# One projection stage of a streaming encoder step: longer steps, an earlier start, and a different share of expert rows on TensorE

## The reference, cut to what matters

```python
h   = x @ w_in                           # q, k, v, gates
x   = LayerNorm(alpha*x + concat(A, B) @ w_out)
# PEER, for each frame: 8 heads, 16 experts each = 128 rows of two tables
sc = einsum('thpd,hpnd->thpn', q, sub_keys); s, i = top_k(sc, 16)
cand = s[:, :, 0, :, None] + s[:, :, 1, None, :]; top, sel = top_k(cand, 16)
g   = softmax(top)
hid = einsum('td,thkd->thk', xs, u_tab[eidx])
a   = g * gelu(hid)
y   = einsum('thk,thkd->td', a, v_tab[eidx])
x   = LayerNorm(alpha*x + y)
```

## Time and profile before

| | |
|---|---|
| median of 3 runs | 1878.59 us (1874.08 to 1881.85) |
| the profiled execution, its time | 1878.59 us |
| its span | 1876.8 us |
| TensorE busy | 1568.1 us, 84% |
| VectorE busy | 1283.8 us, 68% |
| GpSimd busy | 1249.9 us, 67% |
| data moved | 724.85 MB, mean 386 GB/s |
| gathers (queue q0) | 605.75 MB, 82.3% of the 16 engines' span |

### The profile page before, as it was taken

One profiled execution on the slowest core, in us unless ns is written; L12 is line 12 of the kernel. 1 busy time (PEld: TensorE's weight loads), 2 busy tenths in 40 slices (PEclk: granted clock), 3 DMA queues, 4 the chain that ended last, 5 costly groups with the idle time before them and its releaser, 6 DMA issues.

```text
span 1876.8 us, 19183 instructions
## 1 busy us (share of the span) xinstructions
PE 1568.1 (84%) x5552; PEld 825.0 (44%) x5552; DVE 1283.8 (68%) x2826; ACT 609.2 (32%) x1743; POOL 1249.9 (67%) x1199
## 2 busy tenths in 40 slices
PE   8999889979996879877897988887699777767777
PEld 7586445623563545522354553244356222222222
DVE  2279885578957775677787558986756987466543
ACT  1422462222222752223474222245422313122211
POOL 3017676666776775677777657776867777777771
PEclk9999989999998999989998989978899899989999
DMA  9899999998999999999999999999999999999995
GB/s 312 300 350 357 411 384 399 408 396 312 363 410 410 411 409 409 409 410 409 334 405 407 405 401 410 409 349 376 370 399 408 410 409 409 409 409 409 410 410 229
DMA packets 207552, 724.85 MB, mean 386 GB/s; under 512 B 25080, under 2 KB 32024, under 8 KB 207320
## 3 DMA queue, kind: packets, MB, share of 16 engines
q0 software_dynamic: 166720, 605.75, 82.3%
q1 hardware_dynamic: 40728, 117.87, 16.6%
HBM read 716.37 MB, written 7.74 MB: 386 GB/s over the span
## 4 chain that ended last, share of the span: by engine, by line
DMA 29%; POOL 28%; PE 26%; issue 11%; DVE 5%; ACT 1%; SPq 0%; DVEq 0%; POOLq 0%; ACTq 0%
DMA vbuf<-in_peer_v,idx 17%; POOL ubuf L1866 12%; POOL vbuf L1866 11%; PE acc L1058 8%; DMA ubuf<-in_peer_u,idx 5%; POOL wring L1866 3%; PE mixer L1035 3%; PE mixer L759 2%; PE mixer L930 2%; PE mixer L716 2%; POOL held L1866 2%; DMA wring<-in_c_k 2%; PE mixer L872 1%; DVE ubuf L1791 1%; DMA wring<-in_peer_v,idx 1%
## 5 line engine op out<-in xcount | busy, mean ns | idle before, releaser
L1058 PE MATMUL acc<-vbuf,diag 128*128 128x512 f32 x1176 | 599.7, 640 | 152.4 <-DMA vbuf<-in_peer_v,idx 146.7
L1866 POOL DMA_INDIRECT ubuf<-in_peer_u,idx x513 | 549.1, 1070 | 259.5 <-issue 142.1
L1866 POOL DMA_INDIRECT vbuf<-in_peer_v,idx x467 | 507.9, 1087 | 232.4 <-issue 115.3
L1791 DVE CUSTOM_DVE_ANT_0 ubuf<-ubuf,x 128x1024 f32<-128x1024 f32 x329 | 400.0, 1224 | 190.6 <-DMA ubuf<-in_peer_u,idx 187.1
L1058 PEld LDWEIGHTS acc<-vbuf,diag 128*128 128x128 f32 x1176 | 216.0, 200 | 451.7 <-issue 402.7
L1791 DVE CUSTOM_DVE_ANT_0 ubuf<-ubuf,mixer 128x1024 f32<-128x1024 f32 x184 | 223.7, 1218 | 128.1 <-DMA ubuf<-in_peer_u,idx 96.1
L1348 ACT ACTIVATE act_h<-hid 128x4 f32<-128x4 f32 x144 | 29.6, 206 | 525.3 <-DVE hid L1791 524.8
L1803 DVE SCALAR_TENSOR_TENSOR y_acc<-vbuf,coef,y_acc 128x1024 f32<-128x1024 f32 x121 | 155.4, 1285 | 19.9 <-DMA vbuf<-in_peer_v,idx 15.8
L1035 PEld LDWEIGHTS mixer<-stage,wring 128*128 128x128 f32 x1280 | 149.8, 193 | 17.5 <-issue 16.4
L1035 PE MATMUL mixer<-stage,wring 128*128 128x128 f32 x1280 | 151.1, 277 | 2.2 <-DMA wring<-in_w_pq 2.1
L1377 ACT ACTIVATE diag<-ident,coef 128x128 f32<-128x128 f32 x365 | 129.6, 395 | 8.8 <-PE acc L1058 4.8
(11 more groups left out here) (301 smaller groups left out, 2043.8 us busy)
## 6 DMA issues: line engine op xcount, KB each, us to landing
wring<-in_w_pq SPq DMA_DIRECT2D x80, 512.0 KB, 8.1
wring<-in_w_out SPq DMA_DIRECT2D x40, 512.0 KB, 7.4
wring<-in_w_qk SPq DMA_DIRECT2D x34, 512.0 KB, 6.7
ubuf<-in_peer_u,idx POOLq DMA_INDIRECT x513, 11.6
vbuf<-in_peer_v,idx POOLq DMA_INDIRECT x467, 11.6
wring<-in_w_v SPq DMA_DIRECT2D x12, 512.0 KB, 9.7
wring<-in_c_k SPq DMA_DIRECT2D x8, 512.0 KB, 6.3
wring<-in_c_v SPq DMA_DIRECT2D x8, 512.0 KB, 7.6
```

Source lines behind the costliest of these rows:

```text
L1058: last = pe.matmul(sums[hf], diags[D_PLAN[n][0]], v_buf[b][:, hf * 512:(hf + 1) * 512], start=first, stop=last_one)
L1791: nc.vector.tensor_tensor_reduce(out=u, in0=u, in1=x, scale=1.0, scalar=0.0, op0=ALU.mult, op1=ALU.add, accum_out=hid[:, k % MARKS:k % MAR ...
L1866: pool.indirect_dma_start(buf, None, a[table], bass.IndirectOffsetOnAxis(ap=idx[p % 2][:, at:at + 1], axis=0)).then_inc(landed_, 16)
```

## The change

Five things change, and all other code stays.

- Steps of the shared projection: 54 steps become 28. The gate is now one step instead of two, each value tile one step instead of two, each query/key tile one step instead of two.
- Inside a value step the loop over blocks is now outside and the loop over the tile's two input slices inside. The matmuls are the same; those of the 64 sample frames (64 columns of weights instead of 128) come once in a tile instead of twice.
- The stage's range goes from slots 93 to 146 to slots 82 to 144. The later stages of block 2 and `X_MID` start one or two slots sooner, and block 0's n stage two.
- `on_tensor` loses the rule for slots 93 to 145, where every second v row went to TensorE. The general rule holds there now: two of three. Counting by the function, TensorE gets 450 of the 576 v rows instead of 440, and VectorE ten fewer.
- ScalarE's and VectorE's parts of the stage get step numbers to match.

```diff
 def x_steps(p):
-    return {0: 13, 1: 13, SHARED: 54, 3: 2, SMP: 6}[p]
+    return {0: 13, 1: 13, SHARED: 28, 3: 2, SMP: 6}[p]
...
-    if 93 <= k < 146 or 339 <= k < 369:
+    if 339 <= k < 369:
         return k % 2 == 0
     lo, hi = ((62, 82), (70, 122), (51, 111), (41, 105))[p]
     return lo <= at < hi or k % 3 != 2
...
-          2: ((93, 146), (146, 181), (181, 194), (194, 210), (200, 251)),
+          2: ((82, 144), (144, 180), (180, 193), (193, 209), (199, 250)),
...
-X_MID = {1: 26, 2: 146, 3: 257}
+X_MID = {1: 26, 2: 144, 3: 257}
...
-        rows = (211.0, 324.0, 422.0, end + 4.0 + late, end + 4.0 + late)[p]
+        rows = (209.0, 324.0, 422.0, end + 4.0 + late, end + 4.0 + late)[p]
...
-                for c in range(2):
-                    k = 2 * (j % 4) + c
-                    for b, cols in enumerate(XCOLS.values()):
-                        at = (3 * hf + b) * 512
+                for b, cols in enumerate(XCOLS.values()):
+                    at = (3 * hf + b) * 512
+                    for c in range(2):
+                        k = 2 * (j % 4) + c
                         last = pe.matmul(mixer[0:cols.stop - cols.start, at:at + 512], xs[:, k, cols], w[:, c, :],
                                          start=k == 0, stop=k == KT - 1)
-                    if c == 1:
-                        last.then_inc(v_done, 1)
-                    yield
+                last.then_inc(v_done, 1)
+                yield
...
         def shared_scalar(act):
-                if t == 5:
+                if t == 3:
                     act.wait_ge(gate_z, SHARED + 1)
...
-                if t in (11, 19):
-                    hf = t // 8 - 1
+                if t in (6, 10):
+                    hf = t // 4 - 1
...
         def shared_vector(dve, chain):
-                if t == 3:
+                if t == 2:
                     dve.wait_ge(gate_done, SHARED + 1)
...
-                if t == 12:
+                if t == 6:
                     dve.wait_ge(gate_e, SHARED + 1)
                     dve.wait_ge(v_done, 8 * SHARED + 4)
```

More of the change, by code:

```diff
@@ L702, in shared_tensor @@
                 last = pe.matmul(ps_t[0:FOX_HEADS, 0:XN], wg[:, c, :], xs[:, c, :], start=c == 0, stop=c == KT - 1)
-                if c == KT - 1:
-                    last.then_inc(gate_done, 1)
-                if c % 4 == 3:
-                    yield
+            last.then_inc(gate_done, 1)
+            yield
             for j in range(8):
@@ L727, in shared_tensor @@
                     last = pe.matmul(mixer[:, at:at + XN], w[:, c, :], xs[:, c, :], start=c == 0, stop=c == KT - 1)
[L728 to L732, removed]
+                last.then_inc(qk_done, 1)
+                yield
+            for _ in range(x_steps(SHARED) - 9 - MATS):
                 yield
@@ L1081, in shared_scalar @@
             for t in range(x_steps(SHARED)):
-                if t == 5:
+                if t == 3:
                     act.wait_ge(gate_z, SHARED + 1)
                     nc.scalar.activation(gx[2], gx[1], ACT.Exp).then_inc(gate_e, 1)
-                if t == 14:
+                if t == 7:
                     act.wait_ge(gate_u, SHARED + 1)
                     nc.scalar.activation(gx[4], gx[3], ACT.Ln).then_inc(gate_l, 1)
-                if t in (11, 19):
-                    hf = t // 8 - 1
+                if t in (6, 10):
+                    hf = t // 4 - 1
                     act.wait_ge(v_done, 8 * SHARED + 4 * hf + 4)
@@ L1094, in shared_scalar @@
                     nc.scalar.copy(v_wait[:, cols], mixer[0:DEC, at + 2 * 512:at + 3 * 512]).then_inc(shared_out, 1)
-                n = (t - 23) // 4
-                if t % 4 == 3 and 0 <= n < MATS // 2:
+                n = (t - 12) // 2
+                if t % 2 == 0 and 0 <= n < MATS // 2:
                     act.wait_ge(qk_done, MATS * SHARED + 2 * n + 2)
@@ L1422, in shared_vector @@
                     nc.vector.tensor_scalar(u, e, 1.0, None, ALU.add).then_inc(gate_u, 1)
-                if t == 16:
+                if t == 9:
                     dve.wait_ge(gate_u, SHARED + 1)
@@ L1429, in shared_vector @@
                     link(nc.vector.reciprocal(t5, u))
-                if t == 18:
+                if t == 11:
                     link(nc.vector.tensor_tensor(l, l, t5, ALU.mult))
@@ L1434, in shared_vector @@
                     nc.vector.scalar_tensor_tensor(lf_wait, z, 0.0, l, ALU.min, ALU.subtract).then_inc(logf_done, 1)
-                if t == 20:
+                if t == 13:
                     dve.wait_ge(logf_done, SHARED + 1)
```

## The result

| | before | changed |
|---|---|---|
| median | 1876.34 us (4 runs, 1873.78 to 1881.85) | 1897.12 us (4 runs, 1896.46 to 1897.78) |
| profiled execution, time | 1878.59 us | 1893.44 us |
| its span | 1876.8 us | 1891.3 us |
| changed / before | | 1.0107, interval [1.0081, 1.0133] |

The changed kernel is about 20 us slower, 1.1%. The profiled execution shows 14.9 us of them. The forecast was 1892, range 1880 to 1903.

The account below looks back on a forecast made before the run. Gathers filling the DMA engines bound the kernel, so unfilled time is lost. Stage idle rises from 16.6 to 29.0 us (+12.4), plus 1 us jitter: 1876.8 + 13.4 = 1890.2 span, plus 1.8 outside, 1892 us; range 1880 to 1903.

Parts of the forecast that it names:

- The stall: Start of the shared projection: TensorE stands at the gate from 380.5 us until xs lands, taken as 400.
- When xs lands: Load of xs: packet turns with the gathers until these run dry at about 397, then 1.8 us for 1000 packets.
- TensorE's work: Shared projection from the gate on: 74.3 us for 18 slots plus 111.8 for 37, together 186.1 us.
- the clock: TensorE after some 20 us idle: a throttled clock adds 2 us, bounds 0 and 4.
- idle DMA: Stage window of 207.5 us less 178.5 of DMA work: 29.0 us idle, before 16.6, so +12.4 us.
- the queue that is worked off, 7.6 us: DMA work in the stage: issue-to-landing time falls from 15.6 us to 8, counted as 7.6 us of transfers.
- The hidden stall: Rival at the stage's start: 15.6 us of queued DMA covers the wait, xs lands by 385; 1876 us, chance 0.20.
- VectorE's relief: Second stretch of the stage: ten v rows fewer, 12.9 us of VectorE, worth 0 to 3.5 us, taken as 0.
- The filled free time: Rival before the stage: values fill TensorE's 10.4 idle us between 382 and 412.7; 13.9 us faster, 1865, chance 0.06.

Follow-up runs that it names:

- one load: Changed kernel with xs by one load from an input in the tile's order: 1879.07 us, 1.0025; same load in the kernel before: 1872.0 us, 0.9988.
- the start at 93: Changed kernel with the shared projection starting at slot 93 again, all else changed: 1.0158 in a first run, then 1884.85 us, 1.0055 in a second.
- the first occasion: First of three timing occasions for the experiments; every kernel was slower there, the kernel before took 1973.85 us.
- the kernel with eight loads: Changed kernel with xs by eight loads of 1280-byte pieces, 1024 packets instead of 3072; one execution, 1883.44 us.

## Why the prediction was right

**The stall, shown.** The gate began at 399.70 (400 forecast), and stage<-in_xT released the wait. The stall was taken away in two experiments (one load, the start at 93), shortened in two, and made alone in another. It is 13 to 15 of the 20 us.

**When xs lands, shown.** Turns by packet until the gathers are dry, then fast. From 396 to 397 us, at the start of the fast stretch, q1 passes 551 packets, most of them pieces of 256 bytes:

```profile
q1 hardware_dynamic: 551, 0.16, 73.9%
```

That is 73.9% x 16/551 = 21 ns of an engine each, no more than the 28 of the forecast.

**TensorE's work, right in its sum.** The chain of the changed kernel has 5.29 us for each value tile and 0.2 in the row behind it (5.5 forecast), 4.31 for a query/key tile, and the last of them started at 586.0 (588 forecast). The stage from the gate on took 186.7 us; the forecast was 188.1 with the clock. Its two halves were not split as forecast. The value half held 17 v rows and not 15: without the clock's 2.2 us it took 77.7 us instead of 74.3, and the second half 106.7 instead of 111.8. The gate took 6.71 us, at a granted clock of 0.50 until 404 (1.2 GHz of 2.4) and 0.95 behind it, against 4.47 us with one load, where TensorE came to it without the long wait: 2.2 us (2 forecast). The Trainium skill (TensorE: Matmul & The Clock Gate, Part 1) says that an idle array is throttled, and here the trace agrees.

**The term that was mis-sized.** I had 29.0 us of idle DMA for the stage, and the trace shows 36.2. The term "the queue that is worked off, 7.6 us" is the one. I had let the queue end at 8 us from issue to landing; it ended at 10.4, by the gathers of 560 to 586 us (median us from issue to landing):

```profile
ubuf<-in_peer_u,idx POOLq DMA_INDIRECT x10, 10.4
vbuf<-in_peer_v,idx POOLq DMA_INDIRECT x9, 10.4
```

And 57.85 MB of gathers were served from 381.2 to 586.4, 141.1 us at 410 GB/s, where I had 140.8 for 55 slots and 7.6 on top. In that time GpSimd issued 54 u and 54 v gathers of 0.524 MB, 56.6 MB. So 1.2 MB came out of the queue, 3.0 us and not 7.6, and the window held 54 slots and not 55, 2.6 us less. That times from issue to landing made too much of the queue is as I read it: the 15.6 us ahead of the stage had packets of xs in them, one for each of the gathers' own, and they are not all gathers still to be moved. It was not tried by itself. In full: the window was 205.2 us instead of 207.5; the gathers took 141.1 instead of 148.4 of it and the rest (11.42 MB, 27.9 us) instead of 30.1, since I had priced xs by its packets' time and not by its bytes; so 36.2 us are left. With 1.3 us more on the side of before, the profiled stage lost 18.3 us more than before, not 12.4. That the profiled execution came out at 1893.44, 1.4 us from the forecast, is luck to this extent: the stage lost some 5 us more than forecast, and the sample block's attention happened to take 5.6 us less than in the profile of before. The median is 5 us above the forecast.

**The hidden stall, wrong by the same term.** That rival had 1876 for no wait at all. With one load the gate began at 385.31, as in the rival, and the kernel came out at 1.0025: not under the kernel before, but slightly over it. Its two halves lost 16.7 + 1.6 = 18.3 us where the rival had 14. That the first 15 us of a stall are covered by the queue is true of the stall itself (2.3 us lost in it) and false of the whole: the value half behind it lost 31.0 us instead of 16.7. As I read it, it would have worked off the same queue, and found none. Per us of wait the stage lost 0.76 (5.2 us for 6.8) to 0.97 us (17.9 for 18.5).

**The ten rows.** The forecast had them inside its sum and gave VectorE's relief no worth. At a start of 82, with one load, that is shown within some 4 us: with and without them the time is the same. At a start of 93 it isn't settled: the kernel with all the changes but the start takes 1.0055, and the one without the rows, with the range of before and with one load 0.9954; the load alone is 0.9988. This leaves some 0.9% for the rows, the stage's two slots less and the later stages' slots, which no run separates. On the first occasion the rows alone took 0.7% [0.3, 1.1].

**The filled free time.** It failed, even with xs there in time: 1879.07 us with one load, where it had 1865. The time before the stage is free in TensorE, but the slots that lie there bring more v rows to TensorE.

**Not settled.** The timed runs put the change at 20.8 us by medians and the profiled executions at 14.9. The changed kernel's profiled time is its lowest by 3 us, the profiled time of before lies 2.3 us above its median, and the kernel before varies by 8 us between runs. The 7 us that the change costs with one load on both sides are explained in part only, by the v rows in the value half.

## What to carry to other kernels

Before a stage is moved forward, look at what its first instruction waits for and when that lands in the trace of before; a wait that costs nothing today may be covered by the very work that is moved behind it. Small pieces on one DMA queue take turns with large ones on another, so as long as the other queue is full, a load's landing time goes by its number of packets: 3072, 1024 and one piece a partition made 29 to 37, 15 and 8.5 us here. The transfers of the other queue pay for long pieces: two v rows came 4 us late beside the single load. And a queue of transfers hides a stall only if what follows would not have lived off the same queue.

## What the runs showed of the hardware

The equal turns of two DMA queues held for packets of 512, 256 and 1280 bytes and of 10 KB against gathers (469 to 469, 498 to 499 in 400 to 405 us before, 416 to 415, and 58 to 64 in 374 to 376 us with one load). The Trainium skill (DMA: Bandwidth & Descriptors, section Queues, rings and completion order) has the engines switch at packet boundaries, which agrees. I had not expected that the longer pieces would also slow the gathers, whose share fell from 87.6% to 76.7%, in 380 to 385 us of the kernel with eight loads:

```profile
q0 software_dynamic: 415, 1.51, 76.7%
q1 hardware_dynamic: 416, 0.48, 27.1%
```

On one occasion the same gathers ran at 340 to 380 GB/s in many slices where the others had 409, and the kernel before took 1974 us instead of 1874 to 1877. That occasion and the third, where before took 1876.65 us, were on the same chip (number 11), so what made the difference stays open. A comparison of four runs made there was wide enough to hide a change of 1% (the interval of the early start alone is 1.0043 to 1.0237).
